# Moving the shifted weights and the mixers' region from 320 to 256 bytes behind their partners, modulo 512, in a two-layer encoder

## Chip, cores and metric

One core of one Trainium2 chip runs the whole program in one launch. The metric is the device time of that launch in microseconds (us), lower is better. The kernel is written by hand, engine by engine: each engine's instruction stream is in the order in which it is written, and semaphores tie the streams together.

## What is computed

The reference is a two-layer streaming encoder for 512 tokens of width 1024, in float32. Cut to its skeleton:

```python
for layer in range(2):
    h = rms_norm(x, norm_mix_pre[layer])
    m = even_mixer(h, ...) if layer == 0 else odd_mixer(h, positions, ...)
    x = x + rms_norm(m, norm_mix_post[layer])
    h = rms_norm(x, norm_ffn_pre[layer])
    u = causal_dwconv(h @ w_up, conv_w, conv_b)        # 1024 -> 2 x 2816
    f = (gelu(u[..., :2816]) * u[..., 2816:]) @ w_down # 2816 -> 1024
    x = x + rms_norm(f, norm_ffn_post[layer])
```

The even mixer is one projection to 2560 columns, a recurrent branch (convolution, gates, scan), stick-breaking attention with 8 heads, and an output projection. The odd mixer is a projection to 1536 columns, rotary attention in a window of 128 with 16 query heads and 4 key heads, and an output projection.

## The kernel before, in words

**Three products for one.** Every large product is made of float32r matmuls. A number is split into a part that float32r holds exactly (`..._hi`) and the rest (`..._lo`), and `three` issues, for each block of the contraction, hi times hi, hi times lo and lo times hi into the same PSUM bank. In the profile these are the lines L1649, L1650 and L1651; the names behind the arrow are first the operand that streams through the array (moving), then the one that is loaded into it (stationary). Each matmul has its own weight load (PEld) of 128 columns.

**Units and slots.** The weights come in units of 128 partitions x 2048 float32 (1 MB), by DMA from SyncE, into a ring of three slots (`w_raw`). ScalarE copies a unit to `w_hi` (L717), VectorE subtracts to get `w_lo`, which takes the place of `w_raw` (L1131). Some units don't use the ring's slot as it stands: those of `SHIFTED` use the same slot `SHIFT` bytes further on (`w_raw_s`, `w_hi_s`, `w_lo_s`; each slot has `SLOT_PAD` = 512 spare bytes for this), and four units of `OWN_SLOT` have space of their own: the first unit of either up-projection in the region (`w_raw_x`, `w_hi_x`, `w_lo_x`), the last units of the output projections with raw and lo in the idle half of `hx_lo` and hi in the region (`w_hi_o`, `w_hi_e`).

**Columns, halves and tokens.** Most matmuls have 512 moving columns: the activations `hx` (or `g`) move and the weights stand, or, in the last down-projection, the weights move. Around the norms, where only half of the tokens is ready, `first_half`, `out_half` and `down_half` stream 256 tokens at a time, with all of a unit's weights loaded once for each half. Three units (2, 7 and the values of the odd mixer, `U_V`) are computed the other way round, tokens by columns: `half` and `tokens` load 128 tokens of `hx` and stream 256 weight columns. The units that `SHIFTED` names are the ones used with 256 moving columns against `hx` or `g`.

**Where things lie.** The order of the tiles in a partition is fixed by `place`. The first slot begins at byte 16512, whose remainder modulo 512 is 128. The slots, `x`, `hx_hi` and `hx_lo` have sizes and gaps that are multiples of 512, so all of them begin at remainder 128; `begin_at(128)` gives the same remainder to `g_hi` and `g_lo`. Slices that matmuls take of a tile begin whole multiples of 512 bytes into it, so an operand's remainder is its tile's. The shifted tiles begin at remainder 448. The region is the space of `g_hi` and `g_lo` while they are not in use, from `big0` on: `yb_hi`, `yb_lo`, `ya_hi`, `ya_lo`, `y_hi`, `y_lo`, the mixers' own tiles, and the own slots named above. All of it begins at 448 too.

So a matmul of shifted weights against `hx` or `g` has its two operands at remainders 448 and 128, one of an output projection has them at 448 (`y`, `ya`, `yb`) and 128 (`w`), and one of a plain unit has 128 and 128. In the output projections' last units `y` or `ya`, `yb` at 448 meets `w_hi_o` or `w_hi_e` at 448 and `hx_lo` at 128.

Of the kernel before, what the change touches and what calls it, by code (L numbers as in the profile page):

```python
# [86 lines left out]
SW_STEPS = 2 * KV  # L87

SHIFTED = {2, 7, U_UP[0] + 1, U_QKV, U_QKV + 1, U_QKV + 2, U_UP[1] + 1, *(U_DOWN[0] + 9 + c for c in range(3))}
SHIFT = 320  # L90
SLOT_PAD = 512

HALVED = {U_UP[0], U_UP[0] + 1, U_QKV, U_QKV + 1, U_UP[1], U_UP[1] + 1}
# [59 lines left out]
def build(nc, io, out):  # L153
# [9 lines left out]
    def at(name, shape, dt, offset):  # L163
        return nc.alloc_sbuf_tensor_at(name, shape, dt, offset=offset)
# [54 lines left out]
    cv = place("cv", [P, T], F32)  # L219
    begin_at(128)  # L220
    g0 = where[0]
    big0 = g0 + 320

    g_hi = place("g_hi", [P, FT, T], F32R)
    g_lo = place("g_lo", [P, FT, T], F32R)
# [52 lines left out]
    for s in range(RING):  # L278
        a = base + s * (2 * UK * 2 * P * 4 + SLOT_PAD) + SHIFT
        shifted.append((at(f"w_lo_s{s}", [P, UK, 2, P], F32R, a), at(f"w_raw_s{s}", [P, UK, 2, P], F32, a),  # L280
# [1998 lines left out]
```

## Time and profile before

| | us |
|---|---|
| median of 3 runs (lowest to highest) | 1079.46 (1079.14 to 1079.46) |
| profiled execution, its own time | 1078.84 |
| its span, first to last instruction | 1077.1 |
| TensorE matmuls busy | 1067.2 (99%) |
| TensorE weight loads busy | 899.7 (84%) |
| VectorE busy | 678.8 (63%) |
| ScalarE busy | 482.7 (45%) |
| GpSimd busy | 58.8 (5%) |

The busy time of matmuls is a union of overlapping intervals: a matmul's record is longer than the distance to the next one. The distance between the starts of two matmuls is called the pitch below. Where the matmuls are back to back, the mean length of a record rises and falls with the pitch.

### The profile page before, as it was taken

The numbers are of one execution on the slowest core, as the hardware profiler recorded it, in microseconds if no ns is written. First come the engines' busy times: TensorE is split into PE (matmuls) and PEld (weight loads), VectorE is DVE, ScalarE is ACT, GpSimd is POOL, SyncE is SP. The second block draws the span as 40 slices with busy tenths as digits, with TensorE's granted clock in tenths as the row PEclk, the third lists the DMA queues.
The fourth block names the chain that finished last, engine by engine and source line by source line (L and its number), as shares of the span: only waits on it lengthen the run. The fifth ranks groups of instructions, "written<-read, shape, count | busy, mean of one in ns | idle before, by whom it ended". The sixth has DMA issues, their size and how long they took to land.

```text
span 1077.1 us, 14667 instructions
## 1 busy us (share of the span) xinstructions
PE 1067.2 (99%) x5814; PEld 899.7 (84%) x5814; DVE 678.8 (63%) x882; ACT 482.7 (45%) x702; POOL 58.8 (5%) x55
## 2 busy tenths in 40 slices
PE   9999999999999999999999999999999999999997
PEld 7876889988888888888899877998888888888886
DVE  6684876977767676522247777398867676751323
ACT  6454765645343444312245377464434343432221
POOL 0000002300000000001103000230000000000000
PEclk9999999999999999999999999999999999999999
DMA  7331142123232222232232623312323232321322
GB/s 238 118 118 61 58 142 69 65 79 117 79 110 86 103 92 91 95 108 73 104 118 70 180 60 118 117 40 81 116 78 117 78 117 78 117 78 64 112 98 79
DMA packets 23206, 105.61 MB, mean 98 GB/s; under 512 B 4080, under 2 KB 6896, under 8 KB 12528
## 3 DMA queue, kind: packets, MB, share of 16 engines
q1 hardware_dynamic: 23008, 104.84, 28.3%
q8 instruction: 39, 0.64, 0.2%
q14 instruction: 15, 0.12, 0.0%
q10 hardware_dynamic: 144, 0.01, 0.0%
HBM read 98.15 MB, written 2.10 MB: 93 GB/s over the span
## 4 chain that ended last, share of the span: by engine, by line
PE 94%; DVE 3%; ACT 1%; DMA 1%; SPq 1%; issue 0%; DVEq 0%; ACTq 0%
PE ps L1649 30%; PE ps L1651 29%; PE ps L1650 29%; PE ps L1814 1%; PE ps L1840 1%; PE ps L1825 1%; DVE w_lo_s L1131 1%; PE ps L2103 1%; PE ps L2114 1%; DVE hx_lo L1436 1%; PE ps L2130 1%; ACT prob L1084 0%; DMA w_raw<-in_even_w_in 0%; DMA w_raw_s<-in_odd_w_qkv 0%; PE ps L1856 0%
## 5 line engine op out<-in xcount | busy, mean ns | idle before, releaser
L1649 PE MATMUL ps<-hx_hi,w_hi 128*128 128x512 f32 x812 | 320.3, 394 | 0.9 <-DVE w_lo L1154 0.9
L1651 PE MATMUL ps<-hx_hi,w_lo 128*128 128x512 f32 x812 | 316.2, 389 | 0.0
L1650 PE MATMUL ps<-hx_lo,w_hi 128*128 128x512 f32 x812 | 316.1, 389 | 0.0
L1131 DVE TENSOR_TENSOR w_lo<-w_raw,w_hi 128x2048 fp32r<-128x2048 f32 (+1 forms) x74 | 167.7, 2266 | 122.9 <-ACT w_hi L717 122.8
L717 ACT ACTIVATE w_hi<-w_raw 128x2048 fp32r<-128x2048 f32 (+1 forms) x76 | 142.2, 1871 | 107.5 <-DMA w_raw<-in_ffn_w_down 90.6
L1649 PEld LDWEIGHTS ps<-hx_hi,w_hi 128*128 128x128 f32 x812 | 152.4, 188 | 38.1 <-issue 6.0
L1651 PEld LDWEIGHTS ps<-hx_hi,w_lo 128*128 128x128 f32 x812 | 152.4, 188 | 32.1
L1650 PEld LDWEIGHTS ps<-hx_lo,w_hi 128*128 128x128 f32 x812 | 152.5, 188 | 31.0 <-issue 0.5
L993 ACT ACTIVATE cg<-ug,vec 128x512 f32<-128x512 f32 x44 | 35.9, 816 | 136.5 <-DVE ug L1465 136.5
L1474 DVE SCALAR_TENSOR_TENSOR cg<-ug,vec,cg 128x511 f32<-128x511 f32 x88 | 65.8, 748 | 20.4 <-ACT cg L993 20.4
L1005 ACT ACTIVATE g_hi<-cv 128x512 f32 (+1 forms) x44 | 27.8, 632 | 111.1 <-DVE cv L1483 111.1
L1465 DVE TENSOR_TENSOR ug<-ps,rbc 128x512 f32<-128x512 f32 x44 | 30.4, 691 | 71.0 <-PE ps L1651 66.3
L1649 PE MATMUL ps<-w_hi,g_hi 128*128 128x512 f32 x176 | 68.8, 391 | 0.0
L1651 PE MATMUL ps<-w_hi,g_lo 128*128 128x512 f32 x176 | 68.5, 389 | 0.0
L1650 PE MATMUL ps<-w_lo,g_hi 128*128 128x512 f32 x176 | 68.5, 389 | 0.0
L1474 DVE SCALAR_TENSOR_TENSOR cv<-uv,vec,cv 128x511 f32<-128x511 f32 x88 | 65.8, 748 | 0.0
L1485 DVE TENSOR_TENSOR g_lo<-cv,g_hi 128x512 f32 (+1 forms) x44 | 30.5, 693 | 37.0 <-ACT g_hi L1005 37.0
L1649 PE MATMUL ps<-g_hi,w_hi 128*128 128x512 f32 x132 | 51.3, 389 | 0.0
L1650 PE MATMUL ps<-g_lo,w_hi 128*128 128x512 f32 x132 | 51.3, 389 | 0.0
L1651 PE MATMUL ps<-g_hi,w_lo 128*128 128x512 f32 x132 | 51.3, 389 | 0.0
L1131 DVE TENSOR_TENSOR w_lo_s<-w_raw_s,w_hi_s 128x2048 fp32r<-128x2048 f32 (+1 forms) x10 | 24.0, 2398 | 25.2 <-ACT w_hi_s L717 25.2
L1651 PEld LDWEIGHTS ps<-w_hi,g_lo 128*128 128x128 f32 x176 | 33.0, 188 | 6.8
(254 smaller groups left out, 1855.9 us busy)
## 6 DMA issues: line engine op xcount, KB each, us to landing
w_raw<-in_ffn_w_up SPq DMA_DIRECT2D x40, 1024.0 KB, 4.8
w_raw<-in_ffn_w_down SPq DMA_DIRECT2D x16, 1024.0 KB, 4.8
w_raw<-in_even_w_in SPq DMA_DIRECT2D x6, 1024.0 KB, 4.7
w_raw<-in_even_w_out SPq DMA_DIRECT2D x3, 1024.0 KB, 4.7
w_raw_s<-in_odd_w_qkv SPq DMA_DIRECT2D x3, 1024.0 KB, 4.8
w_raw<-in_odd_w_qkv SPq DMA_DIRECT2D x3, 1024.0 KB, 5.6
w_raw<-in_odd_w_o SPq DMA_DIRECT2D x3, 1024.0 KB, 5.5
rsw<-rp SPq DMA_DIRECT2D x40, 64.0 KB, 2.0
```

Of the source, the lines that this page charges most:

```text
L717: act.activation(w_hi[buffer(u)][:, 0:k], w_raw[buffer(u)][:, 0:k], ACT.Copy).then_inc(w_hi_done, 1)
L993: act.activation(cg[:], ug[:], ACT.Identity, scale=col(ffn_vec(layer, 2, j)), bias=col(ffn_vec(layer, 3, j))).then_inc(center, 1)
L1005: act.activation(tile_(g_hi, j), cv[:], ACT.Copy).then_inc(g_hi_done, 1)
L1131: dve.tensor_tensor(w_lo[s][:, 0:k], w_raw[s][:, 0:k], w_hi[s][:, 0:k], ALU.subtract).then_inc(w_lo_done, 1)
L1436: dve.scalar_tensor_tensor(out=hx_lo[:, i, tokens_of(h)], in0=x[:, i, tokens_of(h)], scalar=gain(*pre, i), in1=hx_hi[:, i, tokens_of(h)], ...
L1465: dve.tensor_tensor(halves(ug[:]), out_tile(u, b0, 0), halves(rbc[:]), ALU.mult).then_inc(scaled, 1)
L1474: dve.scalar_tensor_tensor(out=dst[:, s:], in0=src[:, 0:T - s], scalar=col(ffn_vec(layer, 2 - s, j + FT * b)), in1=dst[:, s:], op0=ALU.mul ...
L1485: dve.tensor_tensor(tile_(g_lo, j), cv[:], tile_(g_hi, j), ALU.subtract).then_inc(g_ready, 1)
L1649: pe.matmul(dst, s_hi, r_hi, start=first, stop=False)
L1650: pe.matmul(dst, s_hi, r_lo, start=False, stop=False)
L1651: return pe.matmul(dst, s_lo, r_hi, start=False, stop=last)
L1814: last = pe.matmul(ps[:, c0:c0 + P * (q + 1)], qT[rows, p, P * q:P * q + P], kT[p][rows, 0:P * (q + 1)], start=q > 0, stop=q < 2, skip_gro ...
```

## The change

Two constants. The shifted weights begin 256 bytes behind their slot in place of 320, and the region begins 256 bytes behind `g0` in place of 320. All tiles of both move down by 64 bytes, to remainder 384; nothing else moves, since `where[0] += big0 - g0` only sets the end of the space. No instruction, wait, size or order changes.

```diff
 SHIFTED = {2, 7, U_UP[0] + 1, U_QKV, U_QKV + 1, U_QKV + 2, U_UP[1] + 1, *(U_DOWN[0] + 9 + c for c in range(3))}
-SHIFT = 320
+SHIFT = 256
 SLOT_PAD = 512
...
     begin_at(128)
     g0 = where[0]
-    big0 = g0 + 320
+    big0 = g0 + 256
```

## Rows read from the trace of the kernel before

**Rows 1.** The page: span, busy time, clock, and the chain that ended last.
```profile
span 1077.1 us, 14667 instructions
...
PE 1067.2 (99%) x5814; PEld 899.7 (84%) x5814; DVE 678.8 (63%) x882; ACT 482.7 (45%) x702; POOL 58.8 (5%) x55
...
PEclk9999999999999999999999999999999999999999
...
PE 94%; DVE 3%; ACT 1%; DMA 1%; SPq 1%; issue 0%; DVEq 0%; ACTq 0%
```

**Rows 2.** All matmuls by form: shapes, count, busy us, mean ns of one, idle before.
```profile
L1650 PE MATMUL ps<-hx_lo,w_hi 128*128 128x512 f32 x812 | 316.1, 389 | 0.0
...
L1650 PE MATMUL ps<-hx_lo,w_hi_s 128*128 128x256 f32 x128 | 35.5, 278 | 0.0
...
L1650 PE MATMUL ps<-w_lo_s,hx_hi 128*128 128x256 f32 x96 | 26.8, 279 | 0.0
...
L1650 PE MATMUL ps<-g_lo,w_hi_s 128*128 128x256 f32 x88 | 24.6, 279 | 0.0
...
L1650 PE MATMUL ps<-y_lo,w_hi 128*128 128x256 f32 x64 | 17.8, 279 | 0.0
...
L1650 PE MATMUL ps<-hx_lo,w_hi_x 128*128 128x256 f32 x64 | 17.8, 279 | 0.0
...
L1650 PE MATMUL ps<-yb_lo,w_hi 128*128 128x256 f32 x32 | 8.9, 278 | 0.0
...
L1650 PE MATMUL ps<-ya_lo,w_hi 128*128 128x256 f32 x32 | 8.9, 277 | 0.0
...
L1650 PE MATMUL ps<-y_lo,w_hi 128*128 128x512 f32 x16 | 6.3, 393 | 0.0
...
L1650 PE MATMUL ps<-ya_lo,w_hi_e 128*128 128x256 f32 x16 | 4.5, 281 | 0.0
```

**Rows 3.** Matmuls by form, 202 to 219 us.
```profile
L1650 PE MATMUL ps<-hx_lo,w_hi_s 128*128 128x256 f32 x30 | 8.4, 281 | 0.0
```

**Rows 4.** Matmuls by form, 567.4 to 583 us.
```profile
L1650 PE MATMUL ps<-hx_lo,w_hi_s 128*128 128x256 f32 x46 | 12.7, 276 | 0.0
```

**Rows 5.** Stretches: length, busy us and count of PE, PEld, DVE, ACT, POOL, clock, DMA.
```profile
202.00:218.00 16.00, 16.00 (x138) 16.00 (x137) 15.44 (x26) 10.26 (x18) 8.96 (x7) 1.00 0.01 2
568.00:582.00 14.00, 14.00 (x126) 14.00 (x125) 13.76 (x23) 9.61 (x17) 9.07 (x7) 1.00 0.01 2
...
587.00:597.00 10.00, 10.00 (x87) 10.00 (x86) 7.81 (x10) 3.36 (x6) 0.00 (x0) 1.00 0.64 189
168.00:175.00 7.00, 7.00 (x65) 7.00 (x64) 4.62 (x11) 3.44 (x6) 0.00 (x0) 1.00 0.45 152
```

**Rows 6.** TensorE in order of time, 201.1 to 220.5 us: start, length, instruction.
```profile
201.14 0.47 PE L1649 MATMUL ps<-hx_hi,w_hi_x 128*128 128x256 f32 x1
...
220.41 0.40 PE L1649 MATMUL ps<-hx_hi,w_hi 128*128 128x512 f32 x1
```

**Rows 7.** TensorE in order of time, 710.56 to 729.6 us.
```profile
710.57 0.47 PE L1649 MATMUL ps<-hx_hi,w_hi_x 128*128 128x256 f32 x1
...
729.59 0.40 PE L1649 MATMUL ps<-hx_hi,w_hi 128*128 128x512 f32 x1
```

**Rows 8.** The chain that ended last, 555 to 585 us: start, length, what.
```profile
by line: DVE w_lo_s L1131 26.0%; DVE hx_lo L1436 23.1%; DMA w_raw_s<-in_odd_w_qkv 16.0%; DVE ps L1426 12.9%; DVE x L1432 12.7%; ACT w_hi_s L717 12.4%; issue 3.7%; ACT m L930 1.6%; PE ps L1649 1.6%; PE ps L1706 1.4%; ACT hx_hi L947 1.4%; ACT
...
580.55 3.31 DVE w_lo_s L1131
```

**Rows 9.** VectorE by form: a product in the region, and the split of plain and shifted weights.
```profile
L1559 DVE TENSOR_TENSOR rsw<-rsw,sin_t 128x512 f32<-128x512 f32 x10 | 6.8, 682 | 0.0
...
L1131 DVE TENSOR_TENSOR w_lo<-w_raw,w_hi 128x1536 fp32r<-128x1536 f32 x3 | 5.3, 1759 | 7.9 <-ACT w_hi L717 7.9
...
L1131 DVE TENSOR_TENSOR w_lo_s<-w_raw_s,w_hi_s 128x1536 fp32r<-128x1536 f32 x1 | 1.8, 1759 | 3.7 <-ACT w_hi_s L717 3.7
```

## Prediction, made before the changed kernel was run

> **What bounds the kernel now.** I read the page first, then all matmuls by form, then stretches and the order of time around the norms. The page says that TensorE sets the time: matmuls are busy for 99% of the span, the clock is at its full level (2.4 GHz) throughout, and the chain that ended last is 94% matmuls [rows 1]. A change of addresses removes no instruction, so it can only act on how fast the stream of matmuls runs, or on the few places where something else sets the pace.
>
> The forms show how fast. A plain matmul of 512 columns has a record of 389 ns; those of 256 columns that this change touches have 277 to 279 on average [rows 2]. These averages are mixtures. Between 202 and 219 us every matmul of shifted weights has 281 ns [rows 3]; between 567.4 and 583 us the same form has 276 [rows 4]. Same line, tiles, remainders, clock: two paces. The counts give the pitch. A record lasts about 2.4 pitches, so a stretch shows some 2.4 more matmuls than start in it: 16.00 us / (138 - 2.4) = 118.0 ns, and 14.00 / (126 - 2.4) = 113.3 ns [rows 5]. The slow pace is 4.7 ns or 4% slower; by record lengths it is 5 ns. I take 4.7 and call them slow and fast. Both exist in either direction: shifted weights moving against a standing `hx` run at 10.00 / (87 - 2.4) = 118.2, while `ya` moving against plain weights runs at 7.00 / (65 - 2.4) = 111.8, within one count of 113.3 [rows 5]. At 256 columns weight loads follow each other without a gap too (PEld 16.00 of 16.00), so two streams of reads are always active, and where one stands in a tile relative to the other can matter.
>
> **The change, part by part.** *What it touches.* Per product (L1650 is one of three), by [rows 2]: with the stationary operand 320 ahead of the moving one, 128 + 88 + 64 = 280 forms (`w_hi_s` under `hx`, under `g`, and `w_hi_x`), or 840 matmuls; with it 192 ahead (448 to 128 is -320, which is 192 modulo 512), 96 + 64 + 32 + 32 = 224, or 672 matmuls (`hx` under moving shifted weights, plain weights under `y`, `yb`, `ya`). All 1512 go to a distance of 256. The `hx_lo` third of the last output units goes from 192 to 256 as well, some 60 matmuls that I leave out, and some 96 matmuls of 512 columns (`y`, `ya`, `yb` against plain weights). All else keeps its distance: the rest of the 512 column products and `w_hi_e`, `w_hi_o` under region tiles (both move).
>
> *What they cost now.* Excess over 276 ns, times three products: 384 x 2 + 264 x 3 + 192 x 3 = 2.14 us for the 840 (2.5 ns each), and 288 x 3 + 192 x 3 + 96 x 2 + 96 x 1 = 1.73 us for the 672 (2.6 ns each) [rows 2]. Together 3.9 us. The 512 column ones have 393 against 389: 96 x 4 = 0.4 us at most [rows 2].
>
> *What distance 256 does to it.* The trace has no such pair. The nearest rows lie on both sides of it, 192 and 320, with 2.6 and 2.5 ns of excess. The value between is 2.55 x 1512 = 3.9 us: a change of 0.0 us, which I take. The bound below is that all run fast and the 0.4 us go too: -4.3 us. The bound above is that all run slow: 4.7 x 1512 - 3.9 = +3.2 us. The one row at distance 0, `ya_lo` under `w_hi_e`, has 281 [rows 2], so the farthest neighbour I have costs the slow pace and no more.
>
> *What lies under other work.* The up-projection's first units in layer 0 run from 201.14 to 220.41 us, 19.27, all slow [rows 6]; the same code in layer 1 runs from 710.57 to 729.59, 19.02 [rows 7]. Of its 162 matmuls (11 calls of `first_half` for the first half of the tokens, 16 for the second, six matmuls each) at 4.7 ns = 0.76 us only 0.25 separate the two, because the fast one catches up with VectorE, which has 15.44 us of work in 16.00 there [rows 5]. So 0.5 us of a gain in layer 0 is not had: the bound below becomes -3.8 us. In the other direction, from 555 to 585 us the chain is VectorE, ScalarE and a DMA, with matmuls at 1.6% for the commonest line [rows 8]; the 126 fast matmuls of [rows 5] and a dozen beside them, 0.66 us, can turn slow at no cost, and 0.5 us in layer 1's stretch likewise. The split that ends that stretch takes 3.31 us [rows 8] and would only be waited for less. The bound above becomes +2.0 us.
>
> *Everything else.* VectorE's split of 1536 elements takes 1759 ns for plain and for shifted weights, and a product of 512 elements with one operand in the region and one outside 682 [rows 9]: its pace doesn't follow these remainders, so moving tiles costs it nothing. If I am wrong by 1% it is hidden outside the stretches of [rows 6 to 8], and in them 1% of some 60 us of VectorE is 0.6 us. DMAs write the same bytes; no queue, slot or wait changes.
>
> One rule of the Trainium skill speaks against any effect. "SBUF — State Buffer", section "Who interferes with whom", gives TensorE two independent read ports, one for the moving operand and one for weight loads, and says that it never waits on anyone; by that rule the sum is 0.0 us exactly. The two paces of one form in [rows 3, 4] show that something slows the pair of streams; whether it is their addresses no run has shown yet.
>
> **The rivals.** *(a) All fast.* If what counts is the distance on a circle of 512 bytes, 256 is the farthest from distance 0, which runs slow, and the slow pace may vanish. For it: at 192 and 320 both paces exist, at 0 I see the slow one. Against: the paces change within one form with nothing but time between them, so the entry decides as well. It gives -3.8 us: 1075.7.
>
> *(b) The circle is shorter.* If the reads repeat every 256 bytes or a smaller power of two down to 128, distances 192 and 320 are both odd multiples of 64, while 256 is the same as 0, and every touched matmul runs slow. For it: the form at distance 0 has 281. Against: the plain 512 column products at distance 0 have 389, 4 ns better than at 192 [rows 2], and those 0.4 us would be gained. +2.0 - 0.4 = +1.6 us: 1081.1, still within 0.2%.
>
> *(c) A heavier collision.* Both streams at the same place of a block at once, and a price that no row shows, so I bound it by the nearest: it costs as much again as the slow pace, 9.4 ns for each of 1512. 14.2 - 3.9 = +10.3 us, less 1.2 hidden as above: 1088.6. It makes the kernel slower by 0.2% once the mean excess passes (3.9 + 1.2 + 2.2) / 1512 = 4.8 ns, just beyond the slow pace. Against: even distance 0 has 281.
>
> *(d) Nothing.* Addresses don't matter and every stretch keeps its pace: 1079.5.
>
> **How the numbers follow.** The profiled execution took 1078.84 us, its span 1077.1; the runs have a median of 1079.46, 0.6 above. Sums are differences, so I put them on the median. Forecast: the paces stay mixed as now, 0.0 us, and the 512 column matmuls give back perhaps 0.1: 1079.4, with its own range of +-1.5, since each stretch between two pauses enters one pace or the other, and a long one of 162 matmuls is worth up to 0.76 us. A difference of 0.2% is 2.2 us, about what a measurement of this kernel tells from none. Chances: forecast 0.52, (a) 0.18, (b) 0.18, (c) 0.07, (d) 0.05. Faster: most of (a) and a little of the forecast's edge, 0.20. Slower: (c), a quarter of (b) and a little edge, 0.15. Same: the rest, 0.65. The range reaches to (b) with a margin of 0.5 above and into (a) below, 1076.4 to 1081.6; left out are (c) and about half of (a), some 0.17.
>
> **What the profile after would show.** The touched forms at 256 columns keep means between 276 and 281, with long stretches at one or the other; that is the forecast. All at 276 and the first units of layer 0 near 19.0 us is (a). All at 281, and `y`, `yb`, `ya` at 512 columns with 389, is (b). Means above 281 is (c). The plain 512 column forms at 389, `w_hi_e` at 281 and VectorE's 1759 must stay where they are; if they move, the step that kept them out fails. The prediction is wrong if the pace follows the distance sharply, or if time comes from outside the touched forms.

## The result: 0.4% slower, and every touched matmul at a pace that the kernel before did not have

| | us |
|---|---|
| before, median of 6 runs (lowest to highest) | 1079.70 (1079.14 to 1080.18) |
| after, median of 6 runs | 1083.37 (1083.10 to 1087.00) |
| ratio, with its 95% interval | 1.0041 [1.0032, 1.0051] |
| profiled execution of after, its own time and its span | 1083.25, 1081.5 |

The prediction was 1079.4 (1076.4 to 1081.6), with the most chance on no change. The kernel became slower, by more than 0.2% even at the low end of the interval, and the time lies above the range. Between the two profiled executions the span grew by 4.4 us.

The page of after, with the same lines as [rows 1]:

```profile
span 1081.5 us, 14667 instructions
...
PE 1072.3 (99%) x5814; PEld 905.6 (84%) x5814; DVE 678.8 (63%) x882; ACT 482.9 (45%) x702; POOL 58.7 (5%) x55
...
PEclk9999999999999999999999999999999999999999
...
PE 97%; DMA 1%; ACT 1%; SPq 1%; issue 0%; DVE 0%; DVEq 0%; ACTq 0%
```

The matmuls' busy time rose by 5.1 us, the clock stayed at its full level, VectorE's 678.8 us stayed. The chain is 97% matmuls in place of 94%, and VectorE's 3% are gone from it: where VectorE had set the pace, TensorE now does. Next, the matmuls by form, as in [rows 2]:

```profile
L1650 PE MATMUL ps<-hx_lo,w_hi 128*128 128x512 f32 x812 | 316.1, 389 | 0.0
...
L1650 PE MATMUL ps<-hx_lo,w_hi_s 128*128 128x256 f32 x128 | 36.2, 283 | 0.0
...
L1650 PE MATMUL ps<-w_lo_s,hx_hi 128*128 128x256 f32 x96 | 27.1, 283 | 0.0
...
L1650 PE MATMUL ps<-g_lo,w_hi_s 128*128 128x256 f32 x88 | 24.9, 283 | 0.0
...
L1650 PE MATMUL ps<-hx_lo,w_hi_x 128*128 128x256 f32 x64 | 18.1, 283 | 0.0
L1650 PE MATMUL ps<-y_lo,w_hi 128*128 128x256 f32 x64 | 18.1, 282 | 0.0
...
L1650 PE MATMUL ps<-ya_lo,w_hi 128*128 128x256 f32 x32 | 9.1, 283 | 0.0
...
L1650 PE MATMUL ps<-yb_lo,w_hi 128*128 128x256 f32 x32 | 9.0, 283 | 0.0
...
L1650 PE MATMUL ps<-y_lo,w_hi 128*128 128x512 f32 x16 | 6.3, 393 | 0.0
...
L1650 PE MATMUL ps<-ya_lo,w_hi_e 128*128 128x256 f32 x16 | 4.5, 283 | 0.0
```

The forms that both kept their distance and have 512 columns stay at 389 ns. All others with 256 columns are at 282 to 283, and those were the only changes among the large products. Before, such a form had 276 in one stretch and 281 in another [rows 3, 4]; 283 was in neither. The counts of stretches, read as in [rows 5] (length, busy us and count of PE, PEld, DVE, ACT, POOL, clock, DMA), show the same pace in two places that had differed:

```profile
204.00:219.00 15.00, 15.00 (x127) 15.00 (x126) 14.45 (x25) 9.89 (x17) 8.58 (x7) 1.00 0.00 0
570.00:584.00 14.00, 14.00 (x119) 14.00 (x118) 13.76 (x23) 9.88 (x17) 9.07 (x7) 1.00 0.01 3
```

15.00 / (127 - 2.4) = 120.4 ns and 14.00 / (119 - 2.4) = 120.1, each within one count of 120.0. From the individual starts, with pauses left out, the pitch in after is 119.9 to 120.0 ns for `w_hi_s` under `g`, `w_hi_s` under `hx`, `hx` under `w_hi_s` and `w_hi_x` under `hx`, 119.6 for plain weights under `y`, `ya`, `yb`, and 120.0 for the own slots of the output projections. In before the same averages are, in this order, 116.1, 114.7, 117.8, 115.9, 116.0 and 117.9. So there are at least three paces: 113.3 and 118, of which before was a mixture, and 120.0. The first units of the up-projections, as in [rows 6] and [rows 7], in the order of time:

```profile
202.53 0.47 PE L1649 MATMUL ps<-hx_hi,w_hi_x 128*128 128x256 f32 x1
...
222.16 0.40 PE L1649 MATMUL ps<-hx_hi,w_hi 128*128 128x512 f32 x1
```

```profile
714.37 0.47 PE L1649 MATMUL ps<-hx_hi,w_hi_x 128*128 128x256 f32 x1
...
734.00 0.40 PE L1649 MATMUL ps<-hx_hi,w_hi 128*128 128x512 f32 x1
```

The first pair spans 19.63 us in place of 19.27, the second 19.63 in place of 19.02: both layers now run at one pace. VectorE's forms of [rows 9] did not move:

```profile
L1559 DVE TENSOR_TENSOR rsw<-rsw,sin_t 128x512 f32<-128x512 f32 x10 | 6.8, 681 | 0.0
...
L1131 DVE TENSOR_TENSOR w_lo_s<-w_raw_s,w_hi_s 128x1536 fp32r<-128x1536 f32 x1 | 1.8, 1758 | 3.6 <-ACT w_hi_s L717 3.6
```

**Where the 4.4 us came from.** I matched the matmuls of both traces one to one and added up the increase of pitch of those that follow each other without a pause.

| place in before, us | its matmul starts later in after by | pitches added up so far |
|---|---|---|
| 150.7 | 0.14 | 0.40 |
| 200.7 (past the even mixer's output) | 1.40 | 1.63 |
| 225.8 (past the first up units) | 1.75 | 1.98 |
| 527.8 (the plain units of layer 0) | 1.75 | 1.98 |
| 545.1 (last down units) | 2.05 | 2.28 |
| 580.7 | 3.15 | 3.98 |
| 590.9 | 2.62 | 4.21 |
| 691.2 (past the odd mixer's output) | 3.47 | 4.67 |
| 741.4, and so to the end | 4.41 | 5.99 |

The pitches add up to 6.0 us and the span to 4.4. Through 300 us of plain units nothing is added. Of the 1.6 us that are absorbed, (4.21 - 2.28) - (2.62 - 2.05) = 1.4 us are absorbed between 545 and 591 us, around the second layer's first norms, where the kernel before waited for VectorE, ScalarE and a transfer [rows 8]. In layer 1's first units, from 710.6 to 729.6, pitches add 1.00 us and the start of the next unit moves 0.61, so 0.4 us more are absorbed, in two pauses of before: its matmuls at 723.85 and 725.39 us start within 0.1 us of the end of a VectorE write to `hx_lo` (L1436), 261 and 179 ns behind the matmul before them, and in after both distances are 120 ns. The rest are pauses elsewhere, of either sign.

### The profile page after: what moved, and what is told of

The parts are those of the page before. It is cut to its first block, busy times and chain, and to the rows that moved or that the text cites. A ratio compares the mean times of both kernels' runs of the same rounds, so it can differ in the third digit from the quotient of the medians.

```text
span 1081.5 us, 14667 instructions
## 1 busy us (share of the span) xinstructions
PE 1072.3 (99%) x5814; PEld 905.6 (84%) x5814; DVE 678.8 (63%) x882; ACT 482.9 (45%) x702; POOL 58.7 (5%) x55
## 4 chain that ended last, share of the span: by engine, by line
PE 97%; DMA 1%; ACT 1%; SPq 1%; issue 0%; DVE 0%; DVEq 0%; ACTq 0%
PE ps L1649 31%; PE ps L1650 30%; PE ps L1651 30%; PE ps L1814 1%; PE ps L1840 1%; PE ps L1825 1%; PE ps L2114 1%; PE ps L2103 1%; DMA w_raw<-in_odd_w_o 1%; PE ps L2130 1%; ACT prob L1084 0%; DMA x<-in_x_t 0%; SPq L563 0%; PE ps L1856 0%; PE ps L1722 0%
```

## The experiments

The theory after the result: what counts is the distance from the moving to the stationary operand modulo 256 bytes, 0 costs 120.0 ns a matmul, and 256 is the same as 0. Its rivals: absolute places decide (where a tile lies in the partition), 256 is a collision of its own that 0 does not share, or the pace comes from other engines around the norms. A ratio is against the kernel before, run on the same chip.

### One half of the change at a time

```diff
-SHIFT = 320
+SHIFT = 256
```

> Only the shifted weights move (SHIFT = 256, region at 320 as before). If the pace belongs to the pair of operands, the 936 matmuls of w_s against hx and g turn to 120 ns (records of 283), those of the region keep their mix of 276 and 281, and the time rises by what 936 matmuls give less what VectorE's stretch between 555 and 585 us hides: about +2.5 us. If what matters is where the region lies, nothing changes here.

Measured: 1081.78 us (1080.86 to 1085.37, 5 runs), ratio 1.0034 [1.0021, 1.0048]. Its matmuls by form:

```profile
L1650 PE MATMUL ps<-g_lo,w_hi_s 128*128 128x256 f32 x88 | 24.9, 283 | 0.0
...
L1650 PE MATMUL ps<-hx_lo,w_hi_x 128*128 128x256 f32 x64 | 17.9, 280 | 0.0
L1650 PE MATMUL ps<-y_lo,w_hi 128*128 128x256 f32 x64 | 17.8, 279 | 0.0
```

```diff
-    big0 = g0 + 320
+    big0 = g0 + 256
```

> Only the region moves (big0 at 256, SHIFT = 320 as before). By the theory of pairs the matmuls of y, ya, yb against plain weights and of w_x against hx turn to 120 ns (283) and the w_s forms keep their mix: about +2 us, and the two parts add up to the whole change (+4 us or so). By the rival that one of the two moves carries all of it, one part costs nothing.

Measured: 1081.87 us (1081.24 to 1082.42, 11 runs), ratio 1.0023 [1.0014, 1.0032]. Its matmuls by form:

```profile
L1650 PE MATMUL ps<-g_lo,w_hi_s 128*128 128x256 f32 x88 | 24.6, 279 | 0.0
...
L1650 PE MATMUL ps<-hx_lo,w_hi_x 128*128 128x256 f32 x64 | 18.1, 283 | 0.0
...
L1650 PE MATMUL ps<-y_lo,w_hi 128*128 128x256 f32 x64 | 18.1, 282 | 0.0
```

Each half moves the forms that it touches to 282 or 283 and leaves the others at 277 to 280: with shifted weights alone `w_hi_s` has pitch 119.9, `w_hi_x` 117.1 and plain weights under `y` 115.9; with the region alone 116.0 to 117.8, 119.7 and 119.7. An edit that moves one set of tiles takes the matmuls that use them to 120 ns, and no others. The others don't stay exactly where they were, though their distances do: `w_hi_x` under `hx` goes from 115.9 to 117.1 in the first run, `w_hi_s` under `hx` from 114.7 to 116.0 in the second. The two halves cost 0.34% and 0.23%, whose sum is more than the 0.41% of both, though the intervals allow the sum too. The spans of the profiled executions grew by 1.9 and 2.4 us, together 4.3 of the 4.4 of both.

### Distance 0 in place of 256

```diff
-SHIFT = 320
+SHIFT = 0
...
-    big0 = g0 + 320
+    big0 = g0 + 0
```

> No offset at all: every pair at distance 0. Theory of the short circle (256 bytes or a divisor): the same as distance 256, all 256 column matmuls at exactly 120 ns, records of 283, time as after (1083 to 1084 us). Theory of the circle of 512 bytes, where 256 is a point of its own: the pace differs from 120 ns, probably the 118 of the slow pace.

Measured: 1084.99 us (1083.42 to 1087.12, 4 runs), ratio 1.0048 [1.0032, 1.0063]. The same forms:

```profile
L1650 PE MATMUL ps<-g_lo,w_hi_s 128*128 128x256 f32 x88 | 24.9, 283 | 0.0
...
L1650 PE MATMUL ps<-hx_lo,w_hi_x 128*128 128x256 f32 x64 | 18.1, 283 | 0.0
L1650 PE MATMUL ps<-y_lo,w_hi 128*128 128x256 f32 x64 | 18.1, 282 | 0.0
```

Every class has the pitch that it has in after, 119.7 to 120.0, within a tenth of a nanosecond. Distance 0 and distance 256 are the same. The profiled execution holds one disturbance of its own: in the trace no matmul runs from 562.64 to 565.10 us, and from the fourth matmul behind the pause on 15 come every 213 ns. The view calls the pause "issue", that is, it names no releaser, but the chain behind it can be read against after. The transfer of this unit's weights is issued at 552.59 us here and at 552.61 in after. Here one of its packets of 8 KB takes 1641 ns, where most take 309, and its last packet lands at 559.67; in after that is 557.07. ScalarE's copy to `w_hi_s`, which waits for it, begins at 559.96 in place of 557.51. VectorE's split follows at 562.71 in place of 560.26, and TensorE's next unit at 565.10 in place of 562.64. Each is late by the same 2.45 us, so the pause comes from a transfer that landed late. Why that packet was slow no run shows. The windows view before and after that pause (columns as above):

```profile
547.00:561.00 14.00, 14.00 (x117) 13.95 (x117) 7.90 (x19) 4.97 (x10) 1.36 (x2) 1.00 0.33 106
...
566.00:570.00 4.00, 4.00 (x24) 4.00 (x24) 1.48 (x3) 3.22 (x5) 0.77 (x1) 0.64 0.19 78
```

The granted clock is 0.64 over 566 to 570 us, after an idle 2.46 us; matmuls of 213 ns are matmuls at the lower level, 1.2 GHz. That costs some 2.5 us and 15 x 93 ns = 1.4 us in this one execution, which is the 3.8 us by which its span is above that of after. Its time is 1087.12; two others of the same kernel took 1083.42 and 1083.94, where after lies. The fourth took 1086.04 and has no trace, so what delayed it is open.

### The other order of the two distances

```diff
-SHIFT = 320
+SHIFT = 64
...
-    big0 = g0 + 320
+    big0 = g0 + 192
```

> Distances 64 (w_s standing, hx moving) and 192, with -64 and -192 in the other direction. Short circle of 256 bytes: 64 is the same as 320 and 192 the same as 448, so the w_s forms mix 276 and 281 as before, and the time is within 1 us of before. Circle of 128: as well. Circle of 512: the paces of 64 have no reason to be those of 320.

Measured: 1079.30 us (1078.37 to 1081.68, 10 runs), ratio 1.0002 [0.9993, 1.0012]. Its forms:

```profile
L1650 PE MATMUL ps<-hx_lo,w_hi_s 128*128 128x256 f32 x128 | 35.4, 276 | 0.0
...
L1650 PE MATMUL ps<-w_lo_s,hx_hi 128*128 128x256 f32 x96 | 26.8, 279 | 0.0
...
L1650 PE MATMUL ps<-g_lo,w_hi_s 128*128 128x256 f32 x88 | 24.6, 279 | 0.0
...
L1650 PE MATMUL ps<-y_lo,w_hi 128*128 128x512 f32 x16 | 6.3, 395 | 0.0
```

Here `hx` and `g` stand at 64 from `w_hi_s`, which modulo 256 is the 320 of before. The pitches are 113.8, 116.1 and 117.8, those of before (114.7, 116.1, 117.8) but for the first. The region's two distances have changed places: `w_hi_x` under `hx` has 115.7 at 192 (115.9 at 64 before), plain weights under `y` 115.0 at 64 (116.0 at 192 before). At 512 columns `y` against plain weights has 233.2 ns against 229.8. In sum nothing is gained or lost: 64 and 320 are the same too.

### Both at 256, and every tile 64 bytes further on

```diff
-    base = (nc.sbuf_base + 31) // 32 * 32
+    base = (nc.sbuf_base + 31) // 32 * 32 + 64
...
-    begin_at(128)
+    begin_at(192)
```

and the two constants of the change.

> The whole layout moved up by 64 bytes: plain weights, hx and g at remainder 192, shifted weights and region at 448, distance 256 as in the changed kernel. Theory of distances: the same as the changed kernel, all touched matmuls at 120 ns (records of 283), about 1083.4 us. Theory of absolute places (operands at whole multiples of 128 bytes collide): the pace leaves 120 ns, and the time goes back to about that of before.

Measured: 1083.62 us (1083.24 to 1084.43, 6 runs), ratio 1.0037 [1.0024, 1.0049]; all touched forms at 283 (`w_hi_x` and `w_hi_s` alike), own slots at 120.0. A shift of both operands by 64 bytes changes nothing, so their absolute places don't decide; the distance between them does.

### Distances that no version had: 128 and 96, 32 and 160, 224 and 32

The same two constants, as SHIFT and as the region's offset: 128 and 96, 32 and 160, 224 and 32.

> Shifted weights at distance 128, region at 96. If the reads repeat every 256 bytes, 128 is the farthest point from a collision and the w_s forms run fast or mixed (276 to 281); if every 128 bytes, 128 is the same as 0 and they run at 120 ns (283) as at 0 and 256. Region at 96: no case yet; between 64 and 128, mixed.

Measured: 1082.40 us (1081.48 to 1083.80, 8 runs), ratio 1.0024 [1.0013, 1.0035].

> Shifted weights at distance 32, region at 160. Theory of a block of 64 bytes: a distance of 32 leaves the two streams in the same block half of the time, and the w_s forms run slow or at 120 ns; 160 is clear of it and mixed. Rival (only exact multiples of 128 or 256 collide): 32 is mixed too, 276 to 281.

Measured: 1081.76 us (1081.19 to 1085.77, 10 runs), ratio 1.0027 [1.0016, 1.0038].

> Shifted weights at distance 224, region at 32: the mirror of the run with 32 and 160. If the circle is 256 bytes, 224 standing against moving is the same as 32 the other way round, and each class repeats what its mirror did there. With the signs told apart, the w_s forms under hx at 224 and the y forms over plain weights at -32 agree, and so do the token units at -224 and w_x at 32.

Measured: 1080.34 us (1079.87 to 1081.56, 10 runs), ratio 1.0007 [0.9998, 1.0017].

Pitches by class, in ns, with the distance modulo 256 from moving to stationary in front:

| kernel | `w_s` under `g` and `hx` | `hx` under `w_s` | `w_x` under `hx` | `w` under `y` |
|---|---|---|---|---|
| before | 64: 116.1, 114.7 | 192: 117.8 | 64: 115.9 | 192: 116.0 |
| 128 and 96 | 128: 119.1 to 119.5 | 128: 119.1 to 119.5 | 96: 117.6 | 160: 119.8 |
| 32 and 160 | 32: 118.3, 118.4 | 224: 117.4 | 160: 119.5 | 96: 118.1 |
| 224 and 32 | 224: 116.7, 116.8 | 32: 118.2 | 32: 118.8 | 224: 117.3 |

No smooth curve runs through these. 128 and 160 are nearly as bad as 0, and a bad and a fair distance lie 32 bytes apart (160 and 192, 224 and 256). Which of the two operands is the weights doesn't matter much: the classes that stand at 224 agree within 0.7 ns (116.7 to 117.4), those at 32 within 0.6 (118.2 to 118.8), as the expectation for the mirror said. The hope that 128, the farthest from 0 on a circle of 256, would be fast is refuted.

### Putting the token units at 64 as well

`hx` under shifted weights stands at 192 and has 117.8; `w_hi_s` under `hx` at 64 has 114.7. If 64 is the better, the three units computed tokens by columns should gain from a shift of their own (192, so that stationary minus moving is 64 modulo 256).

```diff
+TOKEN_UNITS = (2, 7, U_QKV + 2)
+TOKEN_SHIFT = 192
...
+    if u in TOKEN_UNITS:
+        return 2 * RING + len(OWN_SLOT) + slot(u)
...
-    for s in range(RING):
-        a = base + s * (2 * UK * 2 * P * 4 + SLOT_PAD) + SHIFT
...
+    for tag, by in (("s", SHIFT), ("t", TOKEN_SHIFT)):
+        for s in range(RING):
+            a = base + s * (2 * UK * 2 * P * 4 + SLOT_PAD) + by
```

> Before with one change: the three token units (w_s moving, hx standing) get an offset of 192 in place of 320, so that the stationary operand stands 64 past the moving one modulo 256 in place of 192. If the sign counts as the runs so far show it (64 better than 192), their 282 neighbours go from 117.8 ns to 114 to 116, and the time falls by 0.5 to 1.1 us; if only the size of the offset counts, they stay at 117.8.

Measured: 1079.32 us (1078.57 to 1080.41, 11 runs), ratio 0.9999 [0.9990, 1.0008]. The form:

```profile
L1655 PE MATMUL ps<-w_lo_t,hx_hi 128*128 128x256 f32 x96 | 26.8, 280 | 0.0
```

By records it is 280 against 279, as if nothing was gained. The individual starts say otherwise: the pitch of these units falls from 117.8 to 116.4 ns, which is worth 0.4 us, and misses the expected 114 to 116. At the same time `w_hi_s` under `hx`, whose distance was left alone, rises from 114.7 to 116.4, which costs 0.6 us. So the time stays, the distance 64 alone does not give the fast pace, and a form's mean record is not a safe measure of its pitch at the level of 1 ns.

> Halves at 64, tokens and region at 192: all pairs of 256 columns stand at 64 modulo 256, but for w_x under hx (192) and the own units. Theory that 64 is the best place: about 114 to 115 ns over all touched classes, 1.5 to 2.5 us faster than before, 0.2% at most. Rival (the entry into a stretch decides between two paces, not the place): a mix as before, within 0.5 us.

That kernel has the token units' own shift and the constants 64 and 192, so all of these pairs are at 64 but `w_hi_x` under `hx`, at 192. Measured: 1078.48 us (1077.48 to 1082.45, 11 runs), ratio 0.9993 [0.9984, 1.0002]. `w_hi_s` under `hx` is at 276, `w_hi_x` and plain weights under `y` at 278, the token units at 281 (pitches 113.6, 115.7, 115.1 and 117.5). The expected gain of 1.5 to 2.5 us did not come. The interval holds 1, so no version here is shown to be faster than the kernel before.

### The plain products of 512 columns taken apart too

```diff
-SHIFT = 320
+SHIFT = 384
...
+    where[0] += 64
     x = place("x", [P, DT, T], F32)
...
-    begin_at(128)
+    begin_at(192)
...
-    big0 = g0 + 320
+    big0 = g0 + 256
```

> x, hx, g and the region 64 bytes further from the ring, shifted weights with them: the 3317 matmuls of 512 columns whose operands were at distance 0 stand at 192 (ring under hx, g) or 64 (w moving over g), the shifted pairs stay at 64 and 192, w_x under hx goes to 0. The few 512 column pairs measured so far run at 226.9 at 0 and 256 and at 229 to 234 elsewhere. If that holds, 2 to 6 ns for each of some 3300: 7 to 20 us slower, though the 256 column pairs gain from the same distance. Rival (0 is bad for either width and 226.9 is already a collision): faster.

Measured: 1089.41 us (1088.96 to 1090.40, 4 runs), ratio 1.0094 [1.0078, 1.0109]. Its 512 column forms (the lines are one further down):

```profile
L1651 PE MATMUL ps<-hx_lo,w_hi 128*128 128x512 f32 x812 | 319.3, 393 | 0.0
...
L1651 PE MATMUL ps<-w_lo,g_hi 128*128 128x512 f32 x176 | 69.3, 394 | 0.0
```

With the plain operands 64 apart their 389 become 393 and 394, except under `w_lo` (389). By pitches the matmuls with `w` under `hx` and under `g`, now at distance 192, go from 227.0 and 226.7 ns to 229.0 and 228.9, and those with `w` moving over `g`, now at 64, from 226.8 to 233.3. That is 2436 x 2.0 + 396 x 2.2 + 528 x 6.5 ns = 9.2 us of the 10.1 by which the span grew; `w_hi_s` under `hx` rose as well, from 114.7 to 117.7 at its old distance of 64, and so did `w_hi_x` and the own slots, now at 0; pauses take up a part of these. The expectation of 7 to 20 us slower holds. What is the worst distance for 256 columns, 0, is the best of those tried for 512.

### The pair alone, all distances, with every other engine idle

The kernel before runs to its end; then, when the last output is written, TensorE goes on alone with float32r matmuls from one slot's `w_hi` against another's. It adds nothing to what the reference computes, and the time of the whole (1401.27 us, span 1399.5) says nothing. The moving operand always begins at the same remainder, and d shifts the stationary one.

```diff
+        def stretch(d, n, width):
+            for k in range(n):
+                c = 256 * (k % 6)
+                pe.matmul(dst[:, 0:width], st[:, c + d // 4:c + d // 4 + 128], mv[:, c:c + width], start=True, stop=True)
...
+        for d in range(0, 512, 16):
+            stretch(d, 48, 256)
+            wide_ones(2)
+        for d in range(0, 256, 32):
+            plain_ones()
+            stretch(d, 48, 256)
...
+        for d in range(0, 257, 32):
+            stretch(d, 24, 512)
+            plain_ones()
```

`wide_ones` are two matmuls of 512 columns, `plain_ones` two of plain float32; they separate the stretches and set what comes ahead of each.

> The kernel before, and behind its last output, with all other engines idle, matmuls on weights that lie in two slots: 48 in a row of 256 columns with the stationary operand d bytes past the moving one, d from 0 to 496 in steps of 16, two of 512 columns between; then d from 0 to 224 in steps of 32 behind two plain float32 matmuls in place of those; then 24 in a row of 512 columns for d from 0 to 256. Its output is that of the reference, its total time says nothing. Theory (a circle of 256 bytes in which the two read streams meet): the pitch at d and d + 256 is the same, 120.0 ns at 0 and 256, lowest (113.3) around 64, and at 512 columns lowest at 0 and 256 (226.7). Rival (the collision comes from other engines' writes, from the norms' stretches or from the hi and lo pattern): with all else idle the pitch doesn't depend on d. If the entry decides between two paces, some d differ between the first and the second list.

The timeline of that trace (start, length of 48 matmuls, what), first list at d = 0, 32, 64, 112, 128, 192, 256, 320, then three of the second list, d = 0, 64, 192:

```profile
1091.58 5.92 PE L2237 MATMUL ps<-w_hi,w_hi 128*128 128x256 f32 x48
...
1103.93 5.84 PE L2237 MATMUL ps<-w_hi,w_hi 128*128 128x256 f32 x48
...
1116.19 5.62 PE L2237 MATMUL ps<-w_hi,w_hi 128*128 128x256 f32 x48
...
1134.36 5.91 PE L2237 MATMUL ps<-w_hi,w_hi 128*128 128x256 f32 x48
...
1140.58 5.86 PE L2237 MATMUL ps<-w_hi,w_hi 128*128 128x256 f32 x48
...
1165.32 5.82 PE L2237 MATMUL ps<-w_hi,w_hi 128*128 128x256 f32 x48
...
1189.81 5.92 PE L2237 MATMUL ps<-w_hi,w_hi 128*128 128x256 f32 x48
...
1214.43 5.62 PE L2237 MATMUL ps<-w_hi,w_hi 128*128 128x256 f32 x48
...
1288.72 6.10 PE L2237 MATMUL ps<-w_hi,w_hi 128*128 128x256 f32 x48
...
1301.88 6.00 PE L2237 MATMUL ps<-w_hi,w_hi 128*128 128x256 f32 x48
...
1328.07 6.00 PE L2237 MATMUL ps<-w_hi,w_hi 128*128 128x256 f32 x48
```

A length less one record of 0.28 us, by 47, is the pitch: 5.92 gives 120.0, 5.62 gives 113.6. From the individual starts, for 256 columns after two matmuls of 512 (the right column: after two of plain float32):

| d modulo 256 | pitch, ns | after float32 |
|---|---|---|
| 0, 112, 144, 160, 240 | 120.0 | 0: 120.0, 160: 119.9 |
| 80, 128 | 118.6, 118.8 | 128: 118.7 |
| 16, 32, 176 | 118.2, 118.4, 118.1 | 32: 118.4 |
| 48, 96, 192 | 117.8, 117.3, 117.8 | 96: 117.4, 192: 117.8 |
| 208, 224 | 116.7 | 224: 116.6 |
| 64 | 113.3 | 64: 117.8 |

d from 256 to 496 gives the same sixteen numbers again, one by one: 320 as 64, 448 as 192, 256 as 0. With 512 columns it is 226.7 at 0, 228.9 at 192, and 231.9 to 234.4 at 32, 64, 96, 128, 160 and 224. At 256 the first ten average 231 ns and the rest 226.7: there the pace of 0 has to be reached first. The stretch at 0 comes behind other matmuls of 512 columns, all others behind float32. In after, `y`, `ya` and `yb` at 512 columns begin in the same way, with five pitches of 228 to 236 ns and then 226 to 227, which is why they average 229.0.

The engines that were busy around the norms are idle here, and the paces of the kernel return: 120.0 at 0, 118.4 at 32 (118.3 in the kernel), 116.7 at 224 (116.7 and 116.8). So no other engine is needed for the cost: it follows the places of TensorE's own two operands, the moving one and the weights. How it arises inside the chip no run shows. Of the eight distances entered in both ways, only d = 64 has two paces, 113.3 behind matmuls of 512 columns and 117.8 behind float32.

## Why the prediction was wrong

**The step that failed** is "What distance 256 does to it". It took the rows on both sides, 192 and 320, and read the value between them, 2.55 ns of excess. The sweep shows that there is no "between": 320 is 64, the circle is 256 bytes long, and 256 is 0 on it. From one step of 16 bytes to the next the pitch changes by up to 5.3 ns, so two neighbours 64 bytes away say nothing about the middle. What the change costs a matmul is the third pace, 120.0 ns, 6.7 above the fast one and 2.0 above the slow.

**The bound above** failed with it, by a reading of the trace. The form `ya_lo` under `w_hi_e` with 281 ns was called the row at distance 0, and so the slow pace was called the most that 0 can cost. But a third of the matmuls in that unit had `hx_lo` at 192, and the three products alternate. When the change moved that third to 256 as well, the same form went to 283: the 281 was the price of the mixture. A pure distance 0 at 256 columns was nowhere in the trace of before. For the same reason two other steps fail: that the `hx_lo` third can be left out, and that `w_hi_e` stays at 281.

**The rivals.** (b) had the mechanism: shorter circle, 256 equal to 0, all touched forms at one pace, and the 512 column ones slightly better (229.8 to 229.0 ns on average). It had the slow pace as its price and said +1.6. (c) had a price beyond the slow pace, at 9.4 ns too high, and set the point at 4.8 ns from which the kernel is slower; the measured 6.7 lies above it. The argument used against (c), "even distance 0 has 281", is the misread row. (a), all fast, is refuted by after; (d), addresses don't matter, by after, by either half and by the sweep. With the right price the prediction's own sum gives 1512 x 6.7 - 3.9 = +6.2 us, some 0.4 for the own slots (192 matmuls, 2 ns each by `ya_lo` under `w_hi_e`), less 0.1 for 512 columns, and less the cover: with the 1.2 us it had assumed, +5.3; with the 1.6 measured, +4.9. The span gave 4.4, and the pitches 6.0 where the sum has 6.5. The present cost, 3.9 us by records, is 4.1 by the pitches of before over 113.3, and the touched matmuls average 119.6 to 120.0 ns, not quite 120.0.

**What held.** The 1512 matmuls that it names changed, beside them only the 192 of the own slots and slightly the 96 of 512 columns, and the plain ones kept 389. VectorE's split stayed at 1758 to 1759 ns and its busy time at 678.8 us. The two covers were where they were put: 1.4 us between 545 and 591 us in place of 0.7, and 0.4 us in layer 1's first units in place of 0.5. The first is larger because the pauses there had more to give than was counted: from one start to the next they took 748 and 807 ns in before, and 269 and 120 in after.

**The rule.** The Trainium skill, "SBUF — State Buffer", "Who interferes with whom", gives TensorE a port for the moving operand and one for weight loads, independent of each other. By it the change would cost 0.0 us. The sweep shows 113.3 to 120.0 ns with nothing changed but the distance of the two and no other engine at work, so for float32r the rule does not hold here, and the measurement decides.

**Open.** Why 64 has two paces, and what in the order of instructions selects one. `w_hi_s` under `hx` always stood at 64 (or 320) in six kernels, and its pitch was 113.6, 113.8, 114.7, 116.0, 116.4 and 117.7 ns; so at this distance the sweep's rule fixes no pace. Each kernel has one trace, so how a mixture differs between executions is not known. The kernel before shows the fast one at 192 too (`ya`, [rows 5]), which the sweep, with its simple order, does not at either entry. Moving `w_hi_x` to a distance of its own was not tried.

## What to carry to other kernels

For streams of float32r with a weight load for each matmul, treat the distance from the moving to the stationary operand, modulo 256 bytes, as a parameter: in these runs 512 columns were fastest at 0, 256 columns were slowest at 0, 112, 144, 160 and 240 and nearly so at 128, and in this kernel 64 and 192 were as good as any. Don't interpolate between two distances, and don't call the row of a form the price of a pair when other pairs run between its records; run the point itself, which takes one constant. And read the shape of a result by the forms first: four microseconds were 1512 matmuls at 283 ns in place of 277 to 279, and nearly every other row unchanged.

## What the runs showed of the chip that was not expected

- The pitch of 256 column float32r matmuls takes values from 113.3 to 120.0 ns with nothing changed but the operands' distance, with period 256 bytes, and a step of 16 bytes can cost 3.3 ns (224 to 240) or 5.3 (64 to 80, behind matmuls of 512 columns).
- 512 columns prefer what 256 columns fare worst with: 226.7 ns at 0, 232 to 234 at most other distances. With (812 + 176 + 132) x 3 plain products, taking them apart costs this kernel 0.9% (1.0094).
- In one execution a single packet of 8 KB took 1641 ns in place of 309, its transfer landed 2.6 us later than in another execution with the same time of issue, and TensorE stood still for 2.46 us; 15 of the matmuls behind the pause came every 213 ns, at a granted clock of 0.64 over 566 to 570 us.
